# Attention steps of a two-layer encoder: VectorE's low parts between the two minima, the next first score ahead of the values, a quarter of the difference on GpSimd

## The reference, cut to what matters

```python
for each of 8 heads, each block of 128 queries:
    s0, s1 = q0 @ k0.T, q1 @ k1.T                # (128, 1024) each, head dim 64
    a = softmax(s0) - lam * softmax(s1)
    o = a @ v                                    # v is (1024, 128)
o = rms_norm(o, subln_g) * (1 - lambda_init)
x = x + o @ w_o
```

## Time and profile before

| | |
|---|---|
| median of 3 runs | 2423.39 us (2420.17 to 2425.74) |
| profiled execution | 2423.46 us, of which the span of the profile is 2421.5 us |
| busy over the span | PE 97%, DVE 56%, ACT 39%, POOL 42% |
| mean granted TensorE clock | 0.992 |
| attention steps | first minimum at 301.7 us, last step's first minimum at 610.9 us |

### The profile page before, as it was taken

One profiled execution on the slowest core, in us unless ns is written; L12 is line 12 of the kernel. 1 busy time (PEld: TensorE's weight loads), 2 busy tenths in 40 slices (PEclk: granted clock), 3 DMA queues, 4 the chain that ended last, 5 costly groups with the idle time before them and its releaser, 6 DMA issues.

```text
span 2421.5 us, 26264 instructions
## 1 busy us (share of the span) xinstructions
PE 2339.0 (97%) x10404; PEld 1910.1 (79%) x10404; DVE 1357.5 (56%) x1240; ACT 940.7 (39%) x1069; POOL 1025.3 (42%) x661
## 2 busy tenths in 40 slices
PE   7899989999999999999999999999999999999997
PEld 6688767777877888888888888888778888888886
DVE  7566799999465555556422233344555555564223
ACT  5112178787444444444311311112454444442112
POOL 1112123333367677765122422223677667742221
PEclk9999999999999999999999999999999999999999
DMA  3553374441222222223422111112222222234222
GB/s 129 171 177 118 135 202 117 108 114 62 91 92 79 78 79 83 92 79 115 180 90 88 48 44 53 43 52 88 95 70 93 81 87 79 79 130 174 89 80 92
DMA packets 73807, 239.54 MB, mean 99 GB/s; under 512 B 8160, under 2 KB 8544, under 8 KB 73696
## 3 DMA queue, kind: packets, MB, share of 16 engines
q1 hardware_dynamic: 73696, 238.01, 30.1%
HBM read 177.16 MB, written 60.82 MB: 98 GB/s over the span
## 4 chain that ended last, share of the span: by engine, by line
PE 76%; issue 13%; DVE 4%; POOL 3%; ACT 2%; DMA 0%; POOLq 0%; DVEq 0%; SPq 0%; ACTq 0%
PE PS L294 35%; PE PS L777 11%; PE PS L779 11%; PE PS L778 11%; PE PS L686 3%; DVE nb L1295 2%; POOL Wst L279 2%; PE PS L664 1%; PE PS L672 1%; PE PS L665 1%; DVE sq L1314 1%; ACT X L987 1%; ACT X L973 1%; POOL X L1646 1%; PE PS L876 0%
## 5 line engine op out<-in xcount | busy, mean ns | idle before, releaser
L279 POOL TENSOR_TENSOR Wst<-Wraw,Wst 128x1024 fp32r<-128x1024 f32 (+1 forms) x111 | 262.6, 2368 | 879.5 <-ACT Wst L273 879.5
L777 PE MATMUL PS<-XB,U 128*128 128x512 f32 x1208 | 472.7, 391 | 6.9 <-POOL U L1640 6.8
L779 PE MATMUL PS<-XB,U 128*128 128x512 f32 x1224 | 478.1, 391 | 0.0
L778 PE MATMUL PS<-XB,U 128*128 128x512 f32 x1208 | 472.0, 391 | 0.0
L294 PE MATMUL PS<-H,Wst 128*128 128x512 f32 x2070 | 470.1, 389 | 0.7 <-POOL Wst L279 0.4
L294 PEld LDWEIGHTS PS<-H,Wst 128*128 128x128 f32 x2070 | 388.4, 188 | 82.1 <-DVE Tv L1432 0.8
L294 PE MATMUL PS<-XGh,Wst 128*128 128x512 f32 x1536 | 419.5, 393 | 23.7 <-POOL Wst L279 12.1
L273 ACT ACTIVATE Wst<-Wraw 128x1024 fp32r<-128x1024 f32 (+1 forms) x111 | 114.0, 1029 | 649.0 <-DMA Wraw<-weights 648.8
L294 PEld LDWEIGHTS PS<-XGh,Wst 128*128 128x128 f32 x1536 | 289.7, 189 | 87.0 <-issue 24.2
L777 PEld LDWEIGHTS PS<-XB,U 128*128 128x128 f32 x1208 | 228.1, 189 | 56.1 <-POOL U L1640 7.7
L779 PEld LDWEIGHTS PS<-XB,U 128*128 128x128 f32 x1224 | 231.0, 189 | 48.1
(11 more groups left out here) (190 smaller groups left out, 3193.9 us busy)
## 6 DMA issues: line engine op xcount, KB each, us to landing
Wraw<-weights SPq DMA_DIRECT2D x79, 512.0 KB, 3.5
U1f<-ups SPq DMA_DIRECT2D x44, 512.0 KB, 4.7
U2f<-ups SPq DMA_DIRECT2D x44, 512.0 KB, 3.7
h_scratch<-Tv SPq DMA_DIRECT2D x44, 512.0 KB, 5.4
Hf<-h_scratch SPq DMA_DIRECT2D x44, 512.0 KB, 4.4
Wraw<-weights SPq DMA_DIRECT2D x32, 448.0 KB, 3.2
x_scratch<-X SPq DMA_DIRECT2D x16, 512.0 KB, 3.2
X<-x_scratch SPq DMA_DIRECT2D x16, 512.0 KB, 7.7
```

The source lines that it names most:

```text
L279: pool.tensor_tensor(w[:, 1, 0:cols], raw[:, 0:cols], w[:, 0, 0:cols].bitcast(F32), ALU.subtract).then_inc(w_lo, 1)
L777: pe.matmul(ps, wh, bh, start=begin, stop=False, skip_group_check=True)
L778: pe.matmul(ps, wh, bl, start=False, stop=False, skip_group_check=True)
L779: ins = pe.matmul(ps, wl, bh, start=False, stop=kp == KP - 1, skip_group_check=True)
```

## The change

It is confined to the attention steps.

- **VectorE**: min 0, low part of block **i-3**, reciprocal, min 1, difference over the first 768 columns only.
- **GpSimd** makes the other 256 columns, as two instructions (product with the coefficient, sum with P0), after `a_done`; a new semaphore `a_rest` tells of it. The transposes and the next first exponential wait for it too.
- **TensorE**: score 1 of block i, `subln_sum`, transposes of i-2, score 0 of block **i+1**, then a part of the values. The values come in four equal parts of 6 matmuls, at lags 6, 7, 8, 9.
- The steps of the group's end move: Square and Copy from lag 8 to 9, the sum with epsilon on GpSimd from 8 to 10, `subln_sum` and Ln/Exp from 9 to 11, `ot` from 10 to 12, `Yh` from 11 to 12, `Yl` from 12 to 13. `z` now shares the buffer of the squares and `ot` that of the copy, so Copy waits for `Yl` of the group before. The epsilon goes into the scale of Square and Ln, so `dg` multiplies by the identity; same shape.
- `P1` has three buffers, not four; `At` has another layout, in which a group's 512 columns are contiguous for the matmul (before: two pieces of 256).
- The load of `W_more` moves on SyncE's queue from ahead of head 2 to behind the reloads of X, with a wait for `pv_done` 15.

The diff, cut to this:

```diff
@@ PE
+                pe.wait_ge(a_rest, i + 1)
                 wait(pe, al_made, i)
                 for t in range(KT):
...
-                for t in (range(0, 3), range(3, 7), range(7, 8))[part]:
+                for t in range(2 * part, 2 * part + 2):
...
-            ahead = {0: (0, (0, 1)), 1: (0, (2, 3)), 4: (0, (4, 5, 6)), 5: (1, (0, 1, 2)), 6: (1, (3, 4, 5, 6))}
+            ahead = {0: (0, (0, 1)), 1: (0, (2, 3)), 5: (0, (4, 5, 6)), 6: (1, (0, 1, 2)), 7: (1, (3, 4, 5, 6))}
...
                 if not tail:
-                    scores(h, i, ii, parity)
+                    scores(i, 1)
...
-                if on(h, ii - 8, tail):
-                    values_of(8, 2)
+                if on(h, ii - 11, tail):
+                    subln_sum(h * 2 + (ii - 11) // 4)
                 if lagged(h, ii - 2, tail):
                     transposes(i - 2, (ii - 2) % QT)
-                if on(h, ii - 9, tail):
-                    subln_sum(h * 2 + (ii - 9) // 4)
-                if on(h, ii - 6, tail):
-                    values_of(6, 0)
-                if on(h, ii - 7, tail):
-                    values_of(7, 1)
+                if not tail and i + 1 < HEADS * QT:
+                    scores(i + 1, 0)
+                for part in range(4):
+                    if on(h, ii - 6 - part, tail):
+                        values_of(6 + part, part)
@@ ACT
                     wait(act, a_done, i - 1)
+                    wait(act, a_rest, i - 1)
                     act.activation(P0[ii % 2], slot(0), ACT.Exp, bias=nb[:, 2 * (ii % 2):2 * (ii % 2) + 1],
...
-                if on(h, ii - 9, tail):
+                if on(h, ii - 11, tail):
...
-                if on(h, ii - 8, tail):
-                    u = h * 2 + (ii - 8) // 4
+                if on(h, ii - 9, tail):
+                    u = h * 2 + (ii - 9) // 4
                     act.wait_ge(pv_done, u + 1)
-                    wait(act, ss_done, u)
-                    act.activation(osq, slot(3)[:, 0:HALF], ACT.Square).then_inc(o_sq, 1)
                     wait(act, o_scaled, u)
+                    act.activation(osq, slot(3)[:, 0:HALF], ACT.Square, scale=(VD * EPS) ** -0.5).then_inc(o_sq, 1)
+                    wait(act, yl_made, u)
                     act.activation(osb, slot(3)[:, 0:HALF], ACT.Copy, scale=lam[:, 5:6]).then_inc(o_copied, 1)
-                if on(h, ii - 11, tail):
-                    u = h * 2 + (ii - 11) // 4
+                if on(h, ii - 12, tail):
+                    u = h * 2 + (ii - 12) // 4
                     act.wait_ge(o_scaled, u + 1)
@@ DVE
                     minimum(i, ii, 0)
+                if lagged(h, ii - 3, tail):
+                    q = (ii - 3) % QT
+                    dve.wait_ge(ah_made, i - 2)
+                    dve.tensor_tensor(a_tile(A_LO, q), slot(2).rearrange("p (t n) -> p t n", n=P),
+                                      a_tile(A_HI, q).bitcast(F32), ALU.subtract).then_inc(al_made, 1)
...
-                    dve.scalar_tensor_tensor(out=P1[q % 4], in0=P1[q % 4], scalar=coef[:, 3:4],
-                                             in1=P0[q % 2], op0=ALU.mult, op1=ALU.add).then_inc(a_done, 1)
-                if lagged(h, ii - 2, tail):
...
+                    dve.scalar_tensor_tensor(out=P1[(i - 1) % 3][:, main_cols], in0=P1[(i - 1) % 3][:, main_cols],
+                                             scalar=coef[:, 3:4], in1=P0[q % 2][:, main_cols], op0=ALU.mult,
+                                             op1=ALU.add).then_inc(a_done, 1)
@@ POOL
-                if ii < QT:
-                    wait(pool, a_done, i)
+                if lagged(h, ii - 1, tail):
+                    q = (ii - 1) % QT
+                    rest = P1[(i - 1) % 3][:, rest_cols]
+                    pool.wait_ge(co_done, 2 * i)
+                    pool.wait_ge(a_done, i)
+                    pool.tensor_tensor(rest, rest, coef[:, 3:4].to_broadcast([P, S // 4]), ALU.mult
+                                       ).then_inc(a_scaled, 1)
+                    pool.wait_ge(a_scaled, i)
+                    pool.tensor_tensor(rest, rest, P0[q % 2][:, rest_cols], ALU.add).then_inc(a_rest, 1)
...
-                if on(h, ii - 10, tail):
-                    u = h * 2 + (ii - 10) // 4
+                if on(h, ii - 12, tail):
+                    u = h * 2 + (ii - 12) // 4
                     pool.wait_ge(z_done, u + 1)
                     pool.wait_ge(o_copied, u + 1)
-                    wait(pool, yl_made, u)
                     pool.tensor_tensor(ot, osb, z, ALU.mult).then_inc(o_scaled, 1)
...
-                if on(h, ii - 8, tail):
-                    u = h * 2 + (ii - 8) // 4
+                if on(h, ii - 10, tail):
+                    u = h * 2 + (ii - 10) // 4
                     pool.wait_ge(dg_done, u + 1)
```

More of the change, by code:

```diff
@@ L132, in build @@
         pos_land = at("pos_land", [P, S], AR + 72 * K, I32)
[L133 to L134 removed]
+        W_more = at("W_more", [P, 2, 1024], AR + 40 * K, F32R)
+        Wraw_more = at("Wraw_more", [P, 1024], AR + 44 * K)
         Wraw = [at(f"Wraw{t}", [P, 1024], ER + 8 * K * t + 4 * K) for t in range(2)]
@@ L188, in q_set @@
             return 2 if h == 0 else parity
[L190 to L196, removed]
-        def a_tile(where, q):
[L200 to L206, removed]
+        At = at("At", [P, 68, HALF], AR + 32 * K, F32R)
+        A_HI, A_LO = (0, 8), (16, 60)
+        on_q = at("on_q", [P, 2, HALF], AR + 80 * K)
+        osq, osb = on_q[:, 0, :], on_q[:, 1, :]
+        z = osq
+        ot = osb
+        dg = at("dg", [P, HALF], ER + 16 * K)[:, :]
+        ident4 = ident.rearrange("p (a n) -> p a n", a=1).to_broadcast([P, 4, P])
+        def a_tile(where, q):
+            b = where[q // 4]
+            return At[:, b:b + 8, q % 4 * P:(q % 4 + 1) * P]
         lams = cu[:, 0:4 * HD]
@@ L243, in build @@
         inv_done, co_done, a_done, t_done = sem("inverse_done"), sem("coef_done"), sem("a_done"), sem("t_done")
+        a_scaled, a_rest = sem("a_rest_scaled"), sem("a_rest_done")
         ah_made, al_made = sem("ah_made"), sem("al_made")
@@ L652, in _, with scores @@
             full_job(pe, T_WO - 1, 1, 0, XGh, XGl)
[L655 to L666, removed]
+            def scores(i, c):
+                h, q, parity = i // QT, i % QT, i // QT % 2
+                if q == 0 and c == 0:
+                    pe.wait_ge(k_in, 128 * (h + 1))
+                    pe.wait_ge(q_in, 64 * (h + 1))
+                wait(pe, e_done, 2 * i + c - 1)
+                for half in range(2):
+                    cols = slice(half * HALF, (half + 1) * HALF)
+                    qs = QQ[q_set(h, parity)][c][:, q * P:(q + 1) * P]
+                    pe.matmul(slot(c)[:, cols], qs, KK[parity][0][c][:, cols], start=True, stop=False)
+                    ins = pe.matmul(slot(c)[:, cols], qs, KK[parity][1][c][:, cols], start=False, stop=True)
+                ins.then_inc(s_done, 1)
             def transposes(i, q):
                 pe.wait_ge(a_done, i + 1)
+                pe.wait_ge(a_rest, i + 1)
                 wait(pe, al_made, i)
                 for t in range(KT):
-                    ins = pe.transpose(slot(2)[:, t * P:(t + 1) * P], P1[q % 4][:, t * P:(t + 1) * P], ident)
+                    ins = pe.transpose(slot(2)[:, t * P:(t + 1) * P], P1[i % 3][:, t * P:(t + 1) * P], ident)
                 ins.then_inc(t_done, 1)
@@ L685, in values @@
                         first, last = t == 0 and w == 0 and m is A_HI, t == KT - 1 and w == 1
-                        ins = pe.matmul(slot(3)[:, 0:HALF], VV[parity][w][:, c], a_group(m, g, t),
+                        ins = pe.matmul(slot(3)[:, 0:HALF], VV[parity][w][:, c], At[:, m[g] + t, :],
                                         start=first, stop=last)
-                if part == 2:
+                if part == 3:
                     ins.then_inc(pv_done, 1)
@@ L739, in _ @@
             pe.wait_ge(rot_read, 2 * HEADS - 1)
-            run_steps(step, 14)
+            scores(0, 0)
+            run_steps(step, 15)
             def dense(d, base):
@@ L985, in step @@
                     act.wait_ge(nb_done, 2 * i + 2)
-                    wait(act, t_done, i - 3)
-                    act.activation(P1[ii % 4], slot(1), ACT.Exp, bias=nb[:, 2 * (ii % 2) + 1:2 * (ii % 2) + 2],
+                    wait(act, t_done, i - 2)
+                    act.activation(P1[i % 3], slot(1), ACT.Exp, bias=nb[:, 2 * (ii % 2) + 1:2 * (ii % 2) + 2],
                                    scale=-1.0, accum_out=rsum[:, 1, ii:ii + 1]).then_inc(e_done, 1)
@@ L1564, in step @@
                     wait(pool, a_done, i - 1)
+                    wait(pool, a_rest, i - 1)
                     pool.tensor_tensor(coef[:, 3:4], coef[:, 1:2], rsum[:, 0, q:q + 1], ALU.mult).then_inc(co_done, 1)
```

48 lines of the change are left out of this document (22 added, 26 removed).

## The result

The change takes **2437.47 us** (median of 5 runs, 2435.18 to 2438.80) against 2422.79 for the kernel before (median of 5): ratio **1.0060, 95% interval 1.0049 to 1.0071**. Forecast were 2438.5 us and a range of 2427 to 2452. The profiled execution has a span of 2435.5 us, 14.0 more than before.

The account below looks back on a forecast made before the run. The waits between VectorE and TensorE, both with less than 19.74 us of work a group, were taken to bound it. Chains of 4.63 + 5.71 + 4.96 + 5.44 = 20.74, +1.00 for 15 groups, gave 2438.5 us, range 2427 to 2452.

Parts of the forecast that it names:

- The group: Four attention steps between first minima: 4.63 + 5.71 + 4.96 + 5.44 = 20.74 us against 19.74, +1.00 for 15 groups.
- the hand-off before the next first exponential: `Yh` waits for `ot` in the same step, with the next exponential behind it: step of 5.71 us, its follower 4.96.
- The pieces: GpSimd's product 0.62 and sum 0.74 us, together 1.40; product bounds 0.52 (half the 512-column time) and 1.30 (the whole).
- Item 1: Transposes wait behind the low part of i-3: a chain of 4.50 us for every step, 4.63 after Ln and Exp.
- Item 4: TensorE's `subln_sum` waits for `sqd` from GpSimd, behind difference and pieces, with transposes and score behind it: step of 5.44 us.
- `a_rest` waits: Transposes and first exponential wait for GpSimd's pieces until about 1.5 us after the step's start, ahead of other chains: nothing.
- The tail: After the last attention steps TensorE has its own work, as before: nothing added.
- cover: Time from `W_more`'s low part being done to its use: shrinks from 5.3 to about 1 us; if gone, 1 to 2 added.
- The clock: TensorE's granted clock in the attention: stays 1.00 though TensorE waits a little more, no price; a window below 1.00 shows error.
- A: Rival, chance 0.10: the hand-offs don't bind, steps hold 4.50 to 4.63, a gain of up to 12 us, about 2413.
- C: Rival, chance 0.09: added and removed waits cancel, no change, 2419 to 2428 us.
- B: Rival, chance 0.15: GpSimd's pieces are held up beside minimum and low part, 0.9 to 1 us each, 15 more, 2453.

Follow-up runs that it names:

- e1: The change with the whole difference back on VectorE and no GpSimd pieces, new order kept: 2416.02 us, ratio 0.9982 to the kernel before.
- e4: The change with 128 instead of 256 columns of the difference on GpSimd: 2428.38 us, ratio 1.0029 to the kernel before.
- e7: The change with 384 instead of 256 columns of the difference on GpSimd: 2449.99 us, ratio 1.0117 to the kernel before.
- e2: The change with `Yh` moved from lag 12 to lag 13, behind the first exponential, pieces kept: 2428.02 us, ratio 1.0031 to the kernel before.
- e5: The kernel before with only GpSimd's 256 columns of the difference and their waits added, all orders as before: 2429.46 us, ratio 1.0032 to the kernel before.
- e3: The change with the low part back at the end of a VectorE step, at lag 2: 2438.24 us, ratio 1.0070 to the kernel before.
- e6: e2 with `subln_sum` also moved behind score 0: ratio 1.0028 to the kernel before.

## Why the prediction was right

- **The group.** Forecast were 20.74 us. A full group takes 20.82; the mean of 12, 20.71, is nearer only because the run-in group is in it. All four steps were within 0.1 us. e1 shows that the share is the cost, e4 and e7 that it goes by the pieces' length. e2 shows the hand-off before the next first exponential, and e5 that most of the cost needs the new order.
- **From the group to the total: two errors that cancel, which is luck.** I took +1.00 for 15 groups and nothing for the tail. The trace has +1.10 for the 12 groups from step 12 to step 60 (13.2 us), 1.9 less than before in the first 12 steps, 1.2 more in the last three, and 4.7 more in the tail, together 17.1. The first `sqd` comes in step 10, the first `subln_sum` in step 11 and the first `ot` in step 12, and seven of the steps before take 4.53 to 4.55 us; I had charged two groups of the first 12 steps with the hand-offs of a full one, about 4 us too much. That nearly makes up for the tail.
- **The pieces**, for which the trace had no row: 0.62 and 0.74 forecast, 0.615 and 0.740 measured, and 1.39 for the two (446.86 to 448.25) against 1.40. The line through 1, 512 and 1024 columns held, and so did `dg` as the model for the product; the Trainium skill's floor of 2.6 cycles (GPSIMD Engine Reference, section 3.1), which gave 0.74 for the product too, does not hold for this product with a broadcast operand. Of the bounds for it the lower end was the near one, as argued.
- **Item 1, the low part ahead of the transposes**: the wait is there (0.24 and 0.27 in two steps of the group), but e3 shows that it costs nothing under the share, and e1 that the order even gains without the share. I priced it as the floor of each step, 4.50. No step of a full group of the change ends on it. The steps ahead of the first group end (4.53 to 4.55) and the shortest of e2 and e6 (4.52, 4.53) lie just above it; what holds those was not tried.
- **Item 4**: `subln_sum` waits, and the chain had the right length (5.44 forecast, 5.40 measured). Where the wait went in e2, the step fell to 4.95, so it did bound that step. That was a side effect of e2, and e6, meant to test this wait, no longer had it.
- **`a_rest` waits: nothing.** From 340 to 610 us of the change ScalarE's first exponential waited 1.8 us in all for the pieces. Right.
- **The tail** was priced at nothing and cost 4.7 us. TensorE is busy 39.4 of its 40.7 us where it was 36.0 of 36.0: with the longer lags more of the values and one more `subln_sum` are still to do when the scores end. The other 1.3 are idle, 1.08 of it a wait for a low part (630.90). e1, without the share, has a tail of 40.2 with a wait of 1.07 at the same place, so 4.2 of the 4.7 belong to the new order and not to the pieces. `W_more` was ready: its low part ended at 663.52 and the matmul began at 664.72, so 1.2 of cover is left of 5.3, as forecast.

```profile
630.90 1.07 PE L675 MATMUL PS<-con,P_last 128*128 128x128 f32 x8 [1.08 <-DVE At L1306]
```

```profile
661.13 2.39 POOL L278 TENSOR_TENSOR W_more<-Wraw_more,W_more 128x1024 fp32r<-128x1024 f32 x1
```

- **The clock.** I put no price on it and named a window below 1.00 as a sign of being wrong: the window 310 to 320 us of the change shows 0.83, in which TensorE has just waited 2.18 us for the end of GpSimd's first pieces (L1580). It is one short spell. The near-exact total (2437.5 against 2438.5) has luck in it here too: the attention grew by 2 us more than forecast, and the rest of the profiled execution was about 4 shorter.
- **The rivals**: A (hand-offs don't bind) and C fell with the timeline. B (pieces held up) fell too: they ran beside minimum and low part and kept to the line of the earlier trace rows, 0.615 and 0.740.

## What to carry to other kernels

Work moved to an idle engine can cost its length on every chain without slack that passes through that engine, however idle it is by share: here a group saved VectorE 1.1 us and paid two chains 1.4 us each. Before giving work away, look for what stands behind the receiving engine in the same step, above all a consumer in front of the next step's first instruction; if there is one, separate producer and consumer by a step first, and see that no shared buffer brings the wait back (e2). Run a change's parts alone: here one part gained and the other lost four times as much. And price the ends of a loop as well as its middle: longer lags made the steps no slower, but left 4 us more in the tail.

## What the runs showed of the hardware that was not expected

- GpSimd's two-operand work on 128 partitions is a straight line down to small pieces: 461, 740 and 1017 ns for 128, 256 and 384 columns, and 400, 615 and 828 with a broadcast operand. So 2.2 and 1.7 ns a column, and 0.18 fixed.
- Two of the short spells near 1.2 GHz fell at the same places of the program in the profiled executions of before and change (some 745 and 1765 us in, 15 later in the change), but last differently; a third came only before. In all it is 8.5 against 3.5 us of lost clock in the windows shown. That alone moves a single execution by several us, a third of the effect measured here; for sizes like these the mean length of a group tells more than one execution's total.
